# Weaving two attentions and half slabs of the gate projection into a delta rule's inverse and scan

## The reference

```python
h = layer_norm(ALPHA * x + 0.5 * swiglu(x, ffn1), ...)
(dn_q, dn_k, dn_v, dn_b, dn_a, dn_z, sw_q, sw_k, sw_v, xa_q, gates) = split(h @ w_in)
o_dn = deltanet_branch(...)            # chunked gated delta rule, 4 heads, chunks of 64
o_sw = sliding_window_attention(...)   # 8 heads of 64, window 128, sinks
o_xa = memory_cross_attention(...)     # 4 heads of 128, 256 memory rows
merged = sum(sigmoid(gates) * einsum('bsnc,ncd->bsnd', (o_dn, o_sw, o_xa), w_branch))
h = layer_norm(ALPHA * h + merged @ w_out, ...)
h = layer_norm(ALPHA * h + 0.5 * swiglu(h, ffn2), ...)
```

## Time and profile before

| | us |
|---|---|
| median of 3 runs | 3378.24 |
| lowest, highest | 3377.48, 3379.80 |
| profiled execution, its own time | 3377.46 |
| its span, first to last instruction | 3375.7 |
| PE busy | 3110.0 (92%) |
| DVE busy | 1542.7 (46%) |
| ACT busy | 622.2 (18%) |

### The profile page before, as it was taken

How to read it: one execution, slowest core, us unless ns; L and a number is a source line. 1 busy time by engine, 2 the same in 40 slices (tenths; PEclk the granted TensorE clock), 3 DMA queues, 4 the chain that set the end, 5 groups by cost and what they waited for, 6 DMA issues and landing times.

```text
span 3375.7 us, 31049 instructions
## 1 busy us (share of the span) xinstructions
PE 3110.0 (92%) x11644; PEld 2028.9 (60%) x11644; DVE 1542.7 (46%) x3708; ACT 622.2 (18%) x1511; POOL 608.4 (18%) x558
## 2 busy tenths in 40 slices
PE   9999997999999999799999988888889988888877
PEld 7857887785784788678677533333337643333322
DVE  1013424200101342421036677777765577777775
ACT  0102113100100211301035211111114421111110
POOL 0010000100100000010001334444340044444432
PEclk9999998999999999899999999999999999999999
DMA  5443321444444333146423899999994399999998
GB/s 215 162 150 126 124 100 60 141 167 157 139 170 149 130 124 113 50 151 237 157 91 119 331 421 418 415 417 419 409 422 177 120 403 421 421 421 409 419 413 352
DMA packets 114918, 830.13 MB, mean 246 GB/s; under 512 B 12880, under 2 KB 13136, under 8 KB 14160
## 3 DMA queue, kind: packets, MB, share of 16 engines
q0 software_dynamic: 73728, 536.90, 38.5%
q1 hardware_dynamic: 39456, 281.29, 23.7%
q10 hardware_dynamic: 1584, 9.95, 0.8%
HBM read 827.05 MB, written 1.05 MB: 245 GB/s over the span
## 4 chain that ended last, share of the span: by engine, by line
PE 67%; DMA 21%; DVE 6%; issue 4%; ACT 1%; POOL 0%; POOLq 0%; DVEq 0%; SPq 0%; ACTq 0%
PE bank L297 28%; DMA arena<-table_uv,idx 21%; PE bank L324 11%; PE bank L1921 9%; PE bank L662 3%; PE bank L1608 2%; PE bank L1793 2%; DVE arena L2502 1%; PE bank L413 1%; PE bank L1859 1%; PE bank L1867 1%; DVE diag L2510 1%; PE bank L378 1%; PE bank L517 1%; DVE arena L2281 1%
## 5 line engine op out<-in xcount | busy, mean ns | idle before, releaser
L1921 PE MATMUL bank<-arena,diag 128*128 128x512 f32 x2048 | 1022.8, 626 | 185.7 <-DVE diag L2510 178.7
L297 PE MATMUL bank<-x,ring 128*128 128x256 f32 x4256 | 931.8, 381 | 8.2 <-DMA ring<-stream 8.2
L297 PEld LDWEIGHTS bank<-x,ring 128*128 128x128 f32 x4256 | 810.8, 191 | 120.0 <-issue 10.1
L1921 PEld LDWEIGHTS bank<-arena,diag 128*128 128x128 f32 x2048 | 362.9, 193 | 721.9 <-DVE diag L2510 452.3
L2502 DVE CUSTOM_DVE_ANT_0 arena<-arena 128x1024 f32<-128x1024 f32 x512 | 625.5, 1222 | 262.0 <-DMA arena<-table_uv,idx 259.1
L2586 POOL DMA_INDIRECT arena<-table_uv,idx x512 | 538.4, 1052 | 937.0 <-PE bank L1921 717.7
L1288 POOL TENSOR_TENSOR x_tok<-arena,ktail 128x1024 f32<-128x1024 f32 (+1 forms) x12 | 26.2, 2184 | 1664.2 <-ACT arena L687 1664.2
L2158 ACT ACTIVATE dots<-dots 128x1 f32<-128x1 f32 x512 | 103.8, 203 | 1091.8 <-DVE dots L2502 1091.4
L324 PE MATMUL bank<-ring,hid 128*128 128x512 f32 x704 | 303.3, 592 | 0.0
L980 DVE SCALAR_TENSOR_TENSOR hid<-o_sw,bank 128x256 f32<-128x256 f32 x88 | 37.0, 421 | 558.5 <-ACT o_sw L707 558.5
L324 PEld LDWEIGHTS bank<-ring,hid 128*128 128x128 f32 x704 | 133.5, 190 | 165.2 <-issue 165.0
(11 more groups left out here) (405 smaller groups left out, 2536.8 us busy)
## 6 DMA issues: line engine op xcount, KB each, us to landing
ring<-stream SPq DMA_DIRECT2D x258, 1024.0 KB, 4.8
arena<-table_uv,idx POOLq DMA_INDIRECT x512
ktail<-ln_rows ACTq DMA_DIRECT2D x6, 1024.0 KB, 6.7
arena<-mem_rows SPq DMA_DIRECT2D x2, 1024.0 KB, 10.5
arena<-stream SPq DMA_DIRECT2D x2, 1024.0 KB, 7.5
sq<-keys ACTq DMA_DIRECT2D x2, 1024.0 KB, 4.7
cst<-consts SPq DMA_DIRECT2D x1, 1547.0 KB, 8.3
cst<-consts SPq DMA_DIRECT2D x1, 1089.0 KB, 14.5
```

The costliest lines, as they stand in the source:

```text
L297: last = mm(out[:, half * T:half * T + T], w[:, half * KC + k, :], rhs[:, k, :], start=(k == 0), stop=(k == KC - 1))
L1921: last = mm(bank[4 + 2 * tt + half][:, :], diag[:, n % DIAGS, :], row_slot(n)[:, D + 512 * half:D + 512 * half + 512], start=(h == 0 and k ...
```

## The change

Layer by layer in the first block, on all engines that take part:
- The gate projection (slabs 13 to 24) is issued in halves, `gate_half(0)` to `gate_half(23)`, each the 16 instructions of 8 blocks, and uses only banks 0 and 1 in turn (`STREAM_BANK`). A slab still counts as done once, behind its second half, and ScalarE copies it once, behind both.
- The attentions have two banks of their own, `ATT` = 2 and 7 (bank 7 held small sums earlier in the layer), two heads or groups at a time.
- The cross attention moves from the scan into the inverse: scores, maxima and exponentials in levels 0 and 1, transposes and outputs in levels 3 to 5.
- The window attention's scores and masks move into the scan, two heads per step. Its transposes and outputs stay behind the scan, now with halves of the gate projection between them; twelve halves lie in the inverse's gaps and beside u and w, five in and right behind the scan, seven in the tail.
- The sigmoids of the gates move between the copies of the window attention's transposes on ScalarE, each waiting for the copies of the gates that it reads.
- Before the merge TensorE waits for `stream_free` of banks 0 and 1, which before stood ahead of the scan.

```diff
+GATES_FROM = 13
+STREAM_BANK = [w % BANKS for w in range(GATES_FROM)] + [w % 2 for w in range(GATES_FROM, WIN_SLABS)]
...
-        ATT = [0, 1, 2, 6]
-        SWA = [2, 6, 0, 1]
+        ATT = (2, 7)
...
+                def gate_half(i):
+
+                    w = GATES_FROM + i // 2
+                    out = bank[STREAM_BANK[w]][:, i % 2 * T:i % 2 * T + T]
+                    if i % 2 == 0:
+                        slab(l, WIN_AT + w)
+                        pe.wait_ge(stream_free[STREAM_BANK[w]].sem, stream_free[STREAM_BANK[w]].at(l, STREAM_USE[w]))
+                    weights = ring[:, (WIN_AT + w) % RING]
+                    for k in range(KC):
+                        last = mm(out, weights[:, i % 2 * KC + k, :], x[:, k, :], start=(k == 0), stop=(k == KC - 1))
+                    if i % 2 == 1:
+                        last.then_inc(slab_done.sem, 1)
...
+                def xa_scores_of(h):
+
+                    if h == 0:
+                        pe.wait_ge(stream_free[2].sem, stream_free[2].at(l, STREAM_BANK.count(2)))
+                    if h >= 2:
+                        pe.wait_ge(xa_exp.sem, xa_exp.at(l, 2 * (h - 1)))
+                    for qt in range(TT):
+                        last = mm(bank[ATT[h % 2]][:, qt * T:qt * T + T], xaq[:, h, qt * P:qt * P + P],
+                                  kmem[:, h, :], start=True, stop=True)
+                    last.then_inc(xa_scores.sem, 1)
...
+                def sw_scores_of(h):
+
+                    i, kv = h % 4, h // 4
+                    if h < 2:
+                        pe.wait_ge(xa_br.sem, xa_br.at(l, h + 1))
+                    else:
+                        pe.wait_ge(sw_masked.sem, sw_masked.at(l, h - 1))
...
+                level_left(0)
+                xa_scores_of(0)
+                xa_scores_of(1)
+                gate_half(0)
+                level_left(1)
+                gate_half(1)
+                level_update(1)
+                xa_scores_of(2)
+                xa_scores_of(3)
+                gate_half(2)
+                level_left(2)
+                gate_half(3)
+                level_update(2)
+                gate_half(4)
+                level_left(3)
+                gate_half(5)
+                level_update(3)
...
+                sw_scores_of(0)
+                sw_scores_of(1)
+                gate_half(11)
...
+                gate_half(12)
                 scan_in(0)
+                sw_scores_of(2)
+                sw_scores_of(3)
                 scan_out(1)
...
+                gate_half(13)
                 scan_in(1)
+                sw_scores_of(4)
+                sw_scores_of(5)
...
+                gate_half(15)
                 scan_in(3)
+                gate_half(16)
...
+                gate_half(17)
+                gate_half(18)
+                gate_half(19)
+                sw_transposes(0)
+                sw_transposes(1)
+                gate_half(20)
+                sw_transposes(2)
+                sw_transposes(3)
+                gate_half(21)
+                sw_transposes(4)
+                sw_transposes(5)
+                gate_half(22)
+                sw_output(0)
+                sw_output(1)
+                gate_half(23)
...
+                def gate_sigmoid(j):
+                    w = GATES_FROM + (3 * j + 2) // 2
+                    act.wait_ge(stream_free[STREAM_BANK[w]].sem, stream_free[STREAM_BANK[w]].at(l, STREAM_USE[w] + 1))
+                    fn(gates[:, 3 * j:3 * j + 3, :], gates[:, 3 * j:3 * j + 3, :],
+                       ACT.Sigmoid).then_inc(gate_sig.sem, 1)
...
+                xa_exps(0)
+                xa_exps(1)
+                copy_left(1)
+                gate_raw(13)
+                xa_exps(2)
+                xa_exps(3)
+                copy_left(2)
...
+                gate_raw(22)
+                sw_copy(0)
+                sw_copy(1)
+                gate_sigmoid(0)
+                gate_sigmoid(1)
+                sw_copy(2)
+                sw_copy(3)
+                gate_sigmoid(2)
+                gate_sigmoid(3)
+                gate_raw(23)
+                sw_copy(4)
+                sw_copy(5)
+                gate_sigmoid(4)
+                gate_sigmoid(5)
+                sw_branch(0)
+                sw_branch(1)
+                gate_sigmoid(6)
+                gate_raw(24)
...
+                xa_max_of(0)
+                xa_max_of(1)
+                level_step(1)
+                xa_max_of(2)
+                xa_max_of(3)
+                level_step(2)
...
                 new_state(0)
+                sw_mask(2)
+                sw_mask(3)
                 new_values(1)
```

More of the change, by code:

```diff
@@ L40 @@
 WIN_SLABS = 25
+GATES_FROM = 13
+STREAM_BANK = [w % BANKS for w in range(GATES_FROM)] + [w % 2 for w in range(GATES_FROM, WIN_SLABS)]
+STREAM_USE = [STREAM_BANK[:w].count(STREAM_BANK[w]) for w in range(WIN_SLABS)]
 BR_SLABS = 6
@@ L212, in first_block @@
         ba_done = sig("ba_done", 1)
-        stream_free = [sig(f"stream_free{b}", len(range(b, WIN_SLABS, BANKS))) for b in range(BANKS)]
+        stream_free = [sig(f"stream_free{b}", STREAM_BANK.count(b)) for b in range(BANKS)]
         conv_done = sig("conv_done", 12)
@@ L531, in tensor @@
                         last.then_inc(ld_done.sem, 1)
[L532 to L544, removed]
@@ new lines, in sw_transposes @@
+                def sw_transposes(grp):
+                    if grp < 2:
+                        pe.wait_ge(sw_p.sem, sw_p.at(l, 2))
+                    else:
+                        pe.wait_ge(sw_tc.sem, sw_tc.at(l, grp - 1))
+                    for b in range(4):
+                        n = 4 * grp + b
+                        last = nc.tensor.transpose(bank[ATT[grp % 2]][:, b * P:b * P + P],
+                                                   prob[:, n * P:n * P + P], c_("ident"))
+                    last.then_inc(sw_t.sem, 1)
@@ new lines, in tensor @@
+                for tt in range(TT):
+                    for h in range(HEADS):
+                        last = mm(bank[3 + tt][:, h * P:h * P + P], Y[:, tt, h], vb[:, tt, h], start=True, stop=True)
+                    last.then_inc(uw_done.sem, 1)
+                for tt in range(TT):
+                    for h in range(HEADS):
+                        last = mm(bank[5 + tt][:, h * P:h * P + P], kbe[:, tt, h], Y[:, tt, h], start=True, stop=True)
+                    last.then_inc(uw_done.sem, 1)
@@ L598, in tensor @@
                 scan_in(1)
+                sw_scores_of(4)
+                sw_scores_of(5)
                 scan_out(2)
[L600 to L608, removed]
+                gate_half(14)
@@ L609, in tensor @@
                 scan_in(2)
+                sw_scores_of(6)
+                sw_scores_of(7)
                 scan_out(3)
[L612 to L621, removed]
+                gate_half(15)
@@ L627, in tensor @@
                        start=True, stop=True).then_inc(o_ms.sem, 1)
[L628 to L649, removed]
+                gate_half(17)
[13 more added lines that the diff above has]
+                gate_half(23)
                 pe.wait_ge(o_ready.sem, o_ready.at(l, 1))
                 pe.wait_ge(sw_br.sem, sw_br.at(l, 2))
+                for b in range(2):
+                    pe.wait_ge(stream_free[b].sem, stream_free[b].at(l, STREAM_BANK.count(b)))
                 branch = (o_dn, o_sw, o_xa)
```

219 lines of the change are left out of this document (135 added, 84 removed).

## The result

| | before | changed |
|---|---|---|
| median of the runs, us | 3377.86 | 3315.47 |
| lowest to highest | 3373.03 to 3379.80 | 3314.93 to 3320.29 |
| profiled execution, span | 3375.7 | 3318.5 |
| stage: first left product to third merge group, layer 0 | 183.30 | 153.63 |

The ratio is 0.9821, 95% interval 0.9804 to 0.9838: 1.8% faster.

A forecast was written before the change was run, and what follows sets the result against it. TensorE, busy for 92% of the span, was taken as the bound. Per layer, idle 22.4 + clock 6.5 + overlap 1.5 - new waits 0.3 + 0.9 gave 29.2 us, 58.1 over both layers: 3319.5 us, range 3315 to 3331.

The forecast's parts named there:

- Idle time: TensorE's idle time in the window of scan and both attentions, 22.4 us per layer, expected to go.
- the overlaps: Overlap of a block with the one before, regained at nine gaps: 9 x 0.17 = 1.5 us per layer.
- six short gaps: TensorE gaps of 0.69 to 1.77 us in the kernel before, all read as steps of the scan.
- Clock: Three slow stretches behind the long gaps of scan and tail return to full clock: 6.5 us per layer, bounds 0 to 6.8.
- Covers: Halves in inverse, scan and tail outlast the waits they cover; slack 2.6 us at level 1, about 2.6 in the tail.
- The scan's three seams: New state under the window scores of two heads in the scan: 0.1 us late at each of three seams, 0.3 us.
- The last seam: Merge waits for the last gate slab's copy: 0.86 us per layer, not to be hidden in this order.
- Sum: Per layer 29.2 us, in layer 1 28.9, together 58.1 us off the profiled 3377.46.
- The range: Whole kernel: 3315 to 3331 us, the forecast's own spread of 3317 to 3326 widened for the rivals.
- Gaps up to 1.8 us left the clock at 1.00: Clock step for the stage: no gap over 0.9 us is left, so the full clock was expected throughout.

The follow-up runs named there:

- Two experiments that take cover away: Changed kernel with five halves moved out of the scan: 3323.73 us; changed kernel with whole slabs ahead of the inverse's updates: 3323.56 us.
- fillers in the old gaps: Kernel before with unread matmuls, or transposes, added in three gaps of scan and tail: 3364.26 us with matmuls, 3363.18 us with transposes.
- hiding the seam: Changed kernel with the last gate half ahead of the window attention's outputs and the merge's wait for o_sw before its second group: 3314.35 us.
- its second: The changed kernel taken again without an edit: 3315.42 us, ratio 0.9819 to the kernel before.

## Why the prediction was right

- *Idle time, 22.4 us per layer, and the overlaps.* Right: the stage's idle time is 0.84 us. Two experiments that take cover away put back the waits that were counted, place by place (scan 3.8 us, behind updates 3.2 with the overlaps). What the sum left out is small: a block behind a wait takes up to 0.1 us longer itself. One reading of the prediction was wrong and changes no number: not all six short gaps are steps of the scan, since one of 0.69 us stands before the window attention's outputs (549.51) and waits for ScalarE's copies of the transposes.
- *Clock, 6.5 us per layer.* Right in mechanism and size: fillers in the old gaps alone brought 5.9 and 6.4 us in layer 0's stage, and 6.2 and 5.6 in layer 1's.
- *Covers.* The slacks of 2.6 us at level 1 and in the tail were found as 2.7 and 2.6. The scan's three seams, priced 0.1 us each, show no idle row, but by the starts the product behind each comes 0.07 us late and takes 0.11 more (1.16 for 1.05), so they cost 0.5 us together for the 0.3 counted:

```profile
461.80 1.05 PE L629 MATMUL bank<-Q,X 128*128 128x128 f32 x8
...
468.41 1.16 PE L629 MATMUL bank<-state_odd,X 128*128 128x128 f32 x8
```

- *The last seam.* Somewhat too small. The 0.86 us forecast were 0.69 of idle time and 0.17 of overlap; the row shows 0.84 without the overlap, and hiding the seam brought 1.1. It could be hidden, by another order than the one the prediction spoke of. The merge starts at 530.00, 0.20 us behind the end of the gate slab's copy, where in before the product at 493.82 started 0.05 behind its copy (the first row is the changed kernel's, the second that of before); what fills that time the profile doesn't show:

```profile
529.20 0.60 ACT L909 ACTIVATE hid<-bank 128x512 f32<-128x512 f32 x1 [2.13 <-PE bank L517]
...
493.17 0.60 ACT L818 ACTIVATE hid<-bank 128x512 f32<-128x512 f32 x1 [8.10 <-PE bank L297]
```

- *Sum.* Stage 154.1 forecast, 153.63 measured; 58.1 us of gain forecast, 58.9 in the trace up to layer 1's merge. The forecast was made from 3377.46; the median of four runs after is 4 us under it. The profiled execution itself took 3320.29, 0.8 us from the forecast. The other three were near 3315.3, as one of before was at 3373.03: executions of one kernel differ by up to 9 us, and one profiled execution can't say which end it stands at. Most of the scatter stands outside the two stages. From the third merge group of layer 1 to the end of the span it is 1962.6 us in before, 1964.3 in the changed kernel's first profile and 1959.9 in its second; between the two stages it is 667.0, 667.0 and 668.7. Over all ten traces of this case the span without the two stages is 3004.0 to 3011.2 us, in no order with the change (3009.3 in before, 3011.2 and 3008.2 in the changed kernel). So the 4 us look like scatter of this kind rather than a term of the sum. That isn't shown for all of them: the two pairs of medians lie 62.4 and 60.6 us apart, and the two stages give 59.1. What makes the rest is open.
- *The range.* The terms alone gave a spread from 3317 to 3326, and the median of 3315.47 lies below it. It is inside the range because the range was drawn 2 us lower than the terms went. That part is luck; the stage's length and the places of its waits are not.
- *One step was too sure.* "Gaps up to 1.8 us left the clock at 1.00" held in before and failed once in each of the two filler runs. It cost nothing here, since no such gap is left.

## What to carry to other kernels

Where the busiest engine is full in one stage and idle in the next, move its independent work, in pieces somewhat longer than the waits that they cover (here by 2.6 us where it was tight), until the second stage has no long wait left. Price each seam as the length of the chain on the other engines minus the cover, from rows of the trace. For every gap, add the overlap with the block before it and a little for the block behind it (0.17 and 0.1 us here), and add the clock behind every long gap as busy time times what was not granted. Buffers that alternate between two banks need such pieces between their uses too.

## What the runs showed of the hardware

- Transposes (f32, 128x128) hold TensorE's clock up as matmuls do: 79 in a row in an otherwise idle stretch, and the 24 behind them took 2.84 us, against 5.07 behind an idle gap. They bring it back too: in before, the 24 transposes stand alone between a gap of 9.55 us and one of 0.69, and the outputs behind them had the full clock:

```profile
549.50:555.20 5.70, 5.62 (x48) 5.43 (x48) 3.17 (x3) 5.69 (x8) 0.00 (x0) 1.00 0.00 0
```

- Behind a gap of 4.17 us the work took 1.5 us longer in one layer and 3.0 in the other; the granted clock was 0.89 in the window 505 to 515 of the first. Behind 7.62 us, in a stretch with another gap of 2.26, it was 0.50, and then 0.65 in the 9 us of outputs behind. Behind the gaps of 0.59 and 1.47 us in the inverse it stayed at 1.00; behind 1.77 us it stayed up in four layers and fell in two, to 0.76 (528 to 532) and 0.57 (1374 to 1378).
- A block of TensorE's that had to wait takes up to 0.1 us longer itself: 1.16 us for 1.05 with eight 128x128 instructions, 2.02 for 1.95 with sixteen.
